# Moving the next layer's modulation set-up into the feed-forward of a four-layer, two-model transformer kernel

## The reference

```python
def first_block(...):
    s_lat, s_ctx = jax.nn.silu(c), jax.nn.silu(c_ctx)
...
    for i in range(DEPTH):
        mod = (s_lat @ w_mod[i] + b_mod[i])[:, None, :]
        sh1, sc1, g1, sh2, sc2, g2 = jnp.split(mod, 6, axis=-1)
        h = rms_norm(x, norm_mix[i]) * (1.0 + sc1) + sh1
        y, yc = token_mixers(h, hc, w_in[i], w_out[i], ...)
        x = x + g1 * y
        h = rms_norm(x, norm_ffn[i]) * (1.0 + sc2) + sh2
        x = x + g2 * swiglu(h, w_gate[i], w_up[i], w_down[i])
    return rms_norm(x, final_norm)
...
def second_block(...):
    for l in range(DEPTH):
        mod = c_act @ w_mod[l] + b_mod[l]
        sh_m, sc_m, g_m, sh_f, sc_f, g_f = jnp.split(mod, 6, axis=-1)
        h = rms_norm_2(x, mix_norm_pre[l]) * (1.0 + sc_m[:, None, :]) + sh_m[:, None, :]
        y = hybrid_mixer(h, ...)
        x = x + g_m[:, None, :] * rms_norm_2(y, mix_norm_post[l])
        h = rms_norm_2(x, ffn_norm_pre[l]) * (1.0 + sc_f[:, None, :]) + sh_f[:, None, :]
        x = x + g_f[:, None, :] * rms_norm_2(swiglu_2(h, w_gate_up[l], w_down[l]), ffn_norm_post[l])
```

## Time and profile before

| | us |
|---|---|
| median of 3 runs (lowest, highest) | 3956.61 (3956.02, 3957.63) |
| the profiled execution's own time | 3965.3 |
| its span, first to last instruction | 3963.5 |
| PE busy in the span | 3520.0 (89%) |
| mean granted TensorE clock in the span | 0.926 |

### The profile page before, as it was taken

One profiled execution on the slowest core, in us unless ns is written; L12 is line 12 of the kernel. 1 busy time (PEld: TensorE's weight loads), 2 busy tenths in 40 slices (PEclk: granted clock), 3 DMA queues, 4 the chain that ended last, 5 costly groups with the idle time before them and its releaser, 6 DMA issues. The chain is left out here.

```text
span 3963.5 us, 49063 instructions
## 1 busy us (share of the span) xinstructions
PE 3520.0 (89%) x20368; PEld 2899.2 (73%) x20368; DVE 1800.1 (45%) x3375; ACT 1058.1 (27%) x1717; POOL 10.7 (0%) x12
## 2 busy tenths in 40 slices
PE   6998998999997988999997974799997993799997
PEld 4987777888886976878875963468886882567886
DVE  3225654333335235544345447653334448654333
ACT  2112443111112222532222222532222322433222
POOL 0000000000000000000000000000000000000000
PEclk9997999999998987999998985899999996699998
DMA  5340101324241310134553310025443320012332
GB/s 190 124 149 1 47 23 53 112 80 136 72 136 45 86 54 25 33 106 149 154 152 104 93 54 1 1 61 173 138 144 122 100 81 0 1 43 85 96 99 72
DMA packets 318718, 336.52 MB, mean 85 GB/s; under 512 B 12025, under 2 KB 233761, under 8 KB 318497
## 3 DMA queue, kind: packets, MB, share of 16 engines
q1 hardware_dynamic: 318496, 333.38, 27.4%
HBM read 329.67 MB, written 3.67 MB: 84 GB/s over the span
## 5 line engine op out<-in xcount | busy, mean ns | idle before, releaser
L1369 DVE TENSOR_TENSOR weights_low<-weights,weights_high 128x1024 fp32r<-128x1024 f32 (+4 forms) x424 | 485.4, 1147 | 1289.4 <-ACT weights_high L1021 1287.5
L1021 ACT ACTIVATE weights_high<-weights 128x1024 fp32r<-128x1024 f32 (+4 forms) x424 | 422.2, 998 | 1421.6 <-PE banks L520 972.4
L917 PE MATMUL banks<-h_high,weights_high 128*128 128x512 f32 (+1 forms) x1760 | 658.4, 374 | 11.8 <-DVE h_low L1381 10.2
L917 PE MATMUL banks<-h_low,weights_high 128*128 128x512 f32 (+1 forms) x1760 | 650.0, 369 | 0.0
L917 PE MATMUL banks<-h_high,weights_low 128*128 128x512 f32 (+1 forms) x1760 | 648.8, 369 | 0.0
L520 PE MATMUL banks<-weights_high,h_high 128*128 128x426 f32 (+3 forms) x1424 | 516.7, 363 | 5.3 <-DVE h_low L1381 5.3
L520 PE MATMUL banks<-weights_high,h_low 128*128 128x426 f32 (+3 forms) x1424 | 509.5, 358 | 0.0
L520 PE MATMUL banks<-weights_low,h_high 128*128 128x426 f32 (+3 forms) x1424 | 509.1, 357 | 0.0
L917 PEld LDWEIGHTS banks<-h_high,weights_high 128*128 128x128 f32 x1760 | 332.8, 189 | 85.0 <-DVE h_low L1381 17.5
L917 PEld LDWEIGHTS banks<-h_high,weights_low 128*128 128x128 f32 x1760 | 332.9, 189 | 55.8
L917 PEld LDWEIGHTS banks<-h_low,weights_high 128*128 128x128 f32 x1760 | 333.2, 189 | 52.2
(11 more groups left out here) (253 smaller groups left out, 3922.3 us busy)
## 6 DMA issues: line engine op xcount, KB each, us to landing
projected<-in_w_mod SPq DMA_DIRECT2D x80, 1024.0 KB, 5.3
weights<-in_w_gate_up SPq DMA_DIRECT2D x88, 512.0 KB, 3.9
weights<-in_w_down SPq DMA_DIRECT2D x80, 512.0 KB, 3.9
weights<-in_w_in SPq DMA_DIRECT2D x80, 426.0 KB, 3.4
weights<-in_w_gate SPq DMA_DIRECT2D x44, 512.0 KB, 6.6
weights<-in_w_up SPq DMA_DIRECT2D x44, 512.0 KB, 7.7
weights<-in_w_mod SPq DMA_DIRECT2D x32, 512.0 KB, 3.9
weights<-in_w_out SPq DMA_DIRECT2D x32, 512.0 KB, 3.6
```

The source lines that it names most:

```text
L917: mm = pe.matmul(bank[:, 0:cnt], wt[:, k, :], x[:, k, a:a + cnt], start=(k == 0 and q == 0), stop=(k == KD - 1 and q == 2))
L1021: act.activation(WH[s_ % 2][:, 0:k * n], slots[j % LAND][:, 0:k * n], ACT.Copy).then_inc(S["w_high"], 1)
L1369: dve.tensor_tensor(WL[s_ % 2][:, 0:k * n], slots[split_of[s_] % LAND][:, 0:k * n], WH[s_ % 2][:, 0:k * n].bitcast(F32), ALU.subtract).the ...
```

## The change

For layers 0, 1 and 2 the kernel now also knows the layer that follows. SP issues the small loads of the following layer (`then_loads`) in the feed-forward, ahead of the first modulation tile. The bias is loaded straight into `ROWS`, and every tile is added to it. The 24 tiles are moved: two follow each of the blocks 0 and 1 (one after the gate product, one after the up product), one follows each later block, none the down product. After the first half of the last down product PE transposes the vectors, the columns and the first pair of gates of the following layer; DVE and ACT copy them out, DVE makes the scales. The second pair of gates is made in the next layer, beside its projection, into banks 6 and 7. So the head of layers 1, 2 and 3 has no small loads and no modulation work left.

The squares move too: behind the last residual adds of layers 0, 1 and 2, ACT squares each tile, and layers 1 and 3 and the final norm don't square at their start. Layer 2 still does, since the final norm changes the residual in front of it. `TMP` and `PO` get other places, with no other effect. Layer 0's head stays as it was. The core of the diff:

```diff
+    def loads(self, w, nxt, VR, BR, PO):
+        out = []
+        for name, a in self.at.items():
+            if a is not None:
+                v = w[name].rearrange("w (f p) -> (w f) p", p=PT)
+                out.append((VR[a:a + v.shape[0], :], v))
+        out += [(VR[self.next + 8 * i:self.next + 8 * i + 8, :], c.rearrange("a (f p) -> (a f) p", p=PT))
+                for i, c in enumerate(nxt["c"] if nxt else ())]
+        for q in range(4):
+            def quarter(v):
+                n = v.shape[-1] // 512
+                return v.rearrange("a (c q n) -> a q c n", q=4, n=PT)[:, q].broadcast_to([32, n, PT])
+            lane = slice(32 * q, 32 * q + 32)
+            out.append((BR[lane, :].rearrange("p (c n) -> p c n", n=PT), quarter(w["b_mod"])))
+            if self.second:
+                out += [(PO[lane, 256 * i:256 * (i + 1)].rearrange("p (c n) -> p c n", n=PT), quarter(w[n]))
+                        for i, n in enumerate(("post1", "post2"))]
+        return out
...
-    TMP = [SC[:, 2 * H_N + 512 * i:2 * H_N + 512 * (i + 1)] for i in range(2)]
+    TMP = [P[:, 4096 + 512 * i:4608 + 512 * i] for i in range(2)]
...
+                first_of_two = n == w["gate_up"][0][0] and a == w["gate_up"][0][1]
+                if m in (1, 2) and first_of_two:
+                    beside[len(weight_units) - 1] = 2 * m - 1
+                elif not first_of_two:
+                    beside[len(weight_units) - 1] = 2 * m if m < 2 else m + 2
         for half in range(2):
             for k in range(m0, m1, 2):
                 cols(w["w_down"], 512 * half, 512, k, min(k + 2, m1))
-            if m1 == KF:
-                beside[len(weight_units) - 1] = KF + half
...
+    def mods_of(m, by):
+        if not nxt:
+            return []
+        if m < 2:
+            return [2 * m + "ad".index(by)]
+        return [m + 2] if by == "d" else []
...
+    then_loads = then.loads(following["w"], following["nxt"], VR, ROWS, PO) if following else []
...
-            pe.wait_ge(S["small"], n_small)
             if start_loads:
+                pe.wait_ge(S["small"], n_small)
                 pe.wait_ge(S["constants"], 16)
-            bank = B.fill(pe, "d")
-            pe.transpose(bank[:, 0:nvec], VR[0:nvec, :], ident[0:nvec, 0:nvec]).then_inc(S["filled"], 1)
+                bank = B.fill(pe, "d")
+                pe.transpose(bank[:, 0:own.count], VR[0:own.count, :], ident[0:own.count, 0:own.count]).then_inc(S["filled"], 1)
...
+            def gates_beside(slot):
+                g = slot if slot < 2 else slot - 4
+                if not start_loads and slot in (0, 1, 6, 7) and g < 2 * R:
+                    if g < 2:
+                        B.free(pe, 6 + g)
+                    mod_gate(side.fill(pe, "a"), 10 + g // R, g % R).then_inc(S["side"], 1)
+            if start_loads:
+                mod_columns((0, 1, 2, 3))
...
-                    ready[m] = B.emptied_by("d")
-                    if nxt:
-                        mod_beside(m)
+                        if by == "d":
+                            ready[m] = B.emptied_by("d")
+                        for i in mods_of(m, by):
+                            mod_beside(i)
                 for half in range(2):
                     product(GH, GL, OUT_T, (m0, GOFF), 512, m0, m1, lambda i: "d", ready)
-                    if nxt and m1 == KF:
-                        mod_beside(KF + half)
+                    if following and (half, m1) == (0, KF):
+                        pe.wait_ge(S["then_loaded"], n_then)
+                        bank = B.fill(pe, "d")
+                        pe.transpose(bank[:, 0:then.count], VR[0:then.count, :], ident[0:then.count, 0:then.count]).then_inc(S["filled"], 1)
+                        pe.wait_ge(S["then_rows"], 1)
+                        mod_columns((0, 1, 2, 3), ROWS)
+                        mod_columns((6, 7, 8, 9), ROWS)
+                        for c in (4, 5):
+                            for r in range(then.rows):
+                                mod_gate(B.fill(pe, "a"), c, r, ROWS).then_inc(S["filled"], 1)
...
                     i = beside[j]
                     if i == 0:
                         sp.wait_ge(S["mod_room"], 1)
+                        for d_, s_ in then_loads:
+                            sp.dma_start(d_, s_).then_inc(S["then_loaded"], 16)
                     else:
                         sp.wait_ge(S["filled"], mod_release[i - 1])
...
-                    if which or i % 2:
+                    if which or i % 2 and not squares:
                         ins = act.activation(XNV[:, t, :], XV[:, t, :], ACT.Square, accum_out=ssq[:, i:i + 1])
-                ins.then_inc(S["squared"], 1)
+                if which or not squares:
+                    ins.then_inc(S["squared"], 1)
...
+                    g = i + 2 * (j - 1)
+                    if not start_loads and j in (1, 2) and i < 2 and g < 2 * R:
+                        bank = side.empty(act, "a", "a")
+                        act.activation(GBV[:, 1, g % R, g // R * 512:g // R * 512 + 512], bank, ACT.Copy).then_inc(S["side_kept"], 1)
...
+                    if following and (half, m1) == (0, KF):
+                        for _ in range(3):
+                            B.empty(act, "d", "a")
+                        mod_gates(range(1), then.rows)
+            if squares_after:
+                act.activation(nm[:, 0:1], ones_col, ACT.Sqrt)
+                for i, t in enumerate(OUT_T):
+                    act.wait_ge(S["x_final"], i + 1)
+                    act.activation(SC[:, D * i:D * (i + 1)], XV[:, t, :], ACT.Square, accum_out=ssq[:, i:i + 1])
...
-                if i % 2 == 0:
-                    copy_out(bank[:, 0:PT], rows)
-                    mod_first[0] = B.emptied_by("d")
-                else:
+                if i == 0:
+                    dve.wait_ge(S["then_loaded"], n_then)
+                elif i % 2:
                     dve.wait_ge(S["emptied_dve"], mod_first[0])
-                    dve.tensor_tensor(rows, rows, bank[:, 0:PT], ALU.add).then_inc(S["emptied_dve"], 1)
+                dve.tensor_tensor(rows, rows, bank[:, 0:PT], ALU.add).then_inc(S["emptied_dve"], 1)
+                mod_first[0] = B.emptied_by("d")
...
+                    for i in mods_of(m, "a"):
+                        mod_tile(i)
                     ahead()
...
+                    for i in mods_of(m, "d"):
+                        mod_tile(i)
+                if following and m1 == KF:
+                    dve.wait_ge(S["emptied_dve"], B.emptied_by("d"))
+                    if then.second:
+                        for i in range(2):
+                            g = ROWS[:, (4 + 6 * i) * PT:(6 + 6 * i) * PT]
+                            ins = dve.tensor_tensor(g, g, PO[:, 256 * i:256 * (i + 1)], ALU.mult)
+                        step(ins)
+                    dve.sem_inc(S["then_rows"], 1)
                 for half in range(2):
                     for k in range(m0, m1, 2):
                         ahead()
-                    outputs(1, half, more=m0 > 0)
-                    if nxt and m1 == KF:
-                        mod_tile(KF + half)
+                    outputs(1, half, m0 > 0, m1 == KF)
+                    if following and (half, m1) == (0, KF):
+                        bank = B.empty(dve, "d", "d")
+                        dve.tensor_copy(VT[:, 0:then.count], bank[:, 0:then.count]).then_inc(S["emptied_dve"], 1)
+                        mod_columns(0, MT_THEN)
+                        mod_columns(1, MT_THEN)
+                        mod_scales(0, then, MT_THEN, AT_THEN)
+                        mod_scales(1, then, MT_THEN, AT_THEN)
+                        for _ in range(2 * then.rows):
+                            B.empty(dve, "a", "d")
...
+        for l in range(2):
+            layer(nc, T, layers[l]["w"], S, False, l == 0, layers[l]["nxt"], start if l == 0 else (), layers[l + 1], l == 1, True)
+            end_of_layer()
...
+        for l in (2, 3):
+            layer(nc, T, layers[l]["w"], S, True, False, layers[l]["nxt"], (), layers[l + 1] if l == 2 else None, l == 3, l == 2)
```

More of the change, by code:

```diff
@@ L253, in layer @@
     PI32 = T["PI"]
[L255 to L258, removed]
+    own = Vectors(second, nxt)
+    then = Vectors(following["second"], following["nxt"]) if following else None
+    V_C, V_CC, V_N1, V_N2, V_QL, V_CB, V_CWT = (own.at[n] for n in ("c", "c_ctx", "norm1", "norm2", "q_latent_norm", "conv_b", "conv_w"))
+    V_NEXT, n_next = own.next, own.n_next
+    MT_THEN = AT_THEN = None
+    if following:
+        MT_THEN = SM[:, 272:272 + 32 * then.rows].rearrange("p (s k r) -> p s k r", s=4, r=then.rows)
+        AT_THEN = SM[:, 336:336 + 16 * then.rows].rearrange("p (s k r) -> p s k r", s=2, r=then.rows)
     weight_units = []
@@ L424, in spans @@
         return out + [(CTX_T * PT, LAT_T * PT, 0)]
[L427 to L442, removed]
+    small_loads = own.loads(w, nxt, VR, ROWS_IN, None) if start_loads else []
```

(43 more changed lines are left out.)

160 lines of the change are left out of this document (62 added, 98 removed).

## The result

The changed kernel takes 3927.47 us (median of 4 runs, 3924.18 to 3929.3), the kernel before 3957.12 (4 runs) beside it: a ratio of 0.9924, 95% interval 0.9911 to 0.9936, so 29.65 us or 0.75% faster. Forecast were 3930.5 and 26.1 us. The profiled execution took 3924.18 us (span 3922.4), 3.3 under its median, where the one of before stood 8.2 over the median beside it; the two spans are thus 41.1 us apart, and some 11.5 of that is no part of the change.

The account below looks back on a forecast made before the run. PE, busy 89% of the span, bounds the kernel. Heads gain 55.5 us, less 1.5, 8.0, 9.2, 6.5, 3.0 and 1.2, leaving 26.1: 3956.6 to 3930.5 us; range 3917 to 3947 (this case 3919 to 3944).

Parts of the forecast that it names:

- Heads: Starts of layers 1 to 3: transposes begin earlier and layer 1 loses a bank wait; 55.5 us gained in all.
- The warm-up: Eight dummy instructions of `warm(4)` opening each head, mostly at half clock: 6.6 us, bounds 3.6 and 7.2.
- A tie: Heads: second weight split done at 8.3 us, DVE's modulation begins at 8.2, so weights cost nothing; bound 2 us per head.
- The squares: Squares moved behind the last adds: about 1.1 us lost in three layers, 2.1 won in the final norm; net -1.2.
- Bank 6: Layers 2 and 3: first gate beside the projection waits for bank 6, 0.75 us each; -1.5 in all.
- Gates beside the projection: Four in layer 1, two each in layers 2 and 3, at 1.0 us each: -8.0.
- Halves: Set-up work between the halves of the last down product: 5.2 us in layer 0, 2.0 each in layers 1 and 2; -9.2.
- Tiles and their chain: Feed-forward blocks: two more tiles in each of three layers, -6.5; tiles 2 and 3 late in layers 1 and 2, -3.0.
- Cold start: Rival: clock falls back or never comes up before the projection, 4.2 us a head lost; 3943 us, chance 0.12.
- No change: Rival: weights replace small loads as the heads' last wait, some 7 us later than summed; 3955 us, chance 0.08.
- slower: Rival: tile and weight loads too slow in blocks 0 and 1 of layers 1 and 2; 3978 us, chance 0.05.
- 23.7 us of moved work: Work PE keeps outside the heads: gates beside the projection 8.0, between the halves 9.2, tiles 6.5.

Follow-up runs that it names:

- run 4: Changed kernel with vector transpose, columns, scales and all gates back in the layer heads; early loads, squares and tiles stay moved: 3932.45 us, ratio 0.9928.
- run 3: Changed kernel without the four dummy products at the start of the blocks of layers 1, 2 and 3: 3926.41 us, ratio 0.9915.
- run 2: Changed kernel with the first two gates beside the projection one slot later: 3924.89 us, ratio 0.9914.
- run 1: Changed kernel with the squares back in the heads and in the final norm: 3928.92 us, ratio 0.9924.
- run 5: As run 4, without the four head dummies, ACT's four gate copies behind modulation steps 2 and 4, layer 1 with four gates beside its projection: 3923.02 us.
- run 6: As run 5, also without the three dummy products between transposes and projection in layers 1 to 3: 3916.26 us, ratio 0.9879.
- experiment 7: Changed kernel again, no edit, in the rounds of run 5 and run 6, for a second profile: 3931.73 us, ratio 0.9917.

## Why the prediction was right, point by point

The mechanism held: each head lost its wait for the small loads, and PE paid for nearly all of the moved work. The 26.1 us lie inside the measured interval (25 to 35). By the steps:

- *Heads.* Forecast were transposes at 6.6 us and the first modulation at 8.2; measured 5.4, 5.5 and 5.1, and 6.8, 8.2 and 6.8. The warm-up was sized too near its upper end: the eight dummies took 5.2 to 5.5 us. The projection of layer 1 came 21.3 us into its block (22 forecast). "A tie" was the right reading of the place: DVE's second split ends just where the modulation starts. But only layer 3 waits for weights there; in layers 1 and 2 the splits queue behind ACT's scaling of the tiles.
- *The squares: the step that failed.* "In the heads of layers 1 and 3 it gains nothing, since `warm(4)` and the splits end last there" overlooked that layer 1 norms six tiles, and that ACT's table load of 1.28 us stands in that head. Its transposes would start at 8.5 instead of 5.4. The move was put at a loss of 1.2 and is a gain of 4.1 with the table load. The tails it lengthens cost 1.5, 1.3 and 1.2 (1.1 forecast); the final norm's block became 2.0 shorter (2.1). This did no harm to the sum, as the heads had been put at the times that hold with the squares moved.
- *Bank 6.* Found, and sized 0.75 instead of 1.2 in each of two layers.
- *Gates beside the projection.* 1.0 each forecast; in layer 1 four of them and the bank wait that vanished came to +1.7 together, so 3.9 or 0.97 each.
- *Halves.* 5.2 us forecast and 5.4 measured in layer 0. In layers 1 and 2 it was 1.0 and 1.5 instead of 2.0. Without the set-up work, layer 1's second half waits 1.23 us for a weight split (run 4), so part of that work was hidden.
- *Tiles and their chain.* 1.2 us for a tile (1.08 and the change of kind). The chain was put at 3.0: one wait of 1.2 in layer 2 is all that came, in both profiles of the changed kernel; it is 0.8 in run 3, 0.2 in run 2 and nothing in runs 1, 4, 5 and 6. The tile had landed 6.8 us after its issue, where its neighbours need 5.2 to 5.3. Why there alone is open.
- *Rivals.* Cold start: fallen by run 3 in its price, since each projection starts with the full clock. The falling back between the transposes and the projection that it named is there in layer 1, but there the kernel before has it too. The Trainium skill (TensorE: Matmul & The Clock Gate, Part 1: The HAM clock gate) has the throttled clock as the default, released by sustained activity. The rows agree: 0.53 over 2137.5 to 2141 in layer 2's head, full clock behind it; what I made of it was wrong, since in run 3 the clock rose during the transposes alone. No change and slower: the first weights were split from 3.7 to 5.3 us on, and the tiles of layers 1 and 2 landed in 5 to 7 us.

What the prediction did not see is that its two parts are not one: it charged 23.7 us of moved work as the price of the early loads. Of these, 17.2 are the gates and the work between the halves. Run 4 puts that work back into the head and is as fast, and run 6 shows that PE's idle time in the head hides most of it. The tiles' 6.5 stay in every run.

## What to carry to other kernels

When a head waits for small loads and then works on them, move the loads first and measure; the work may fit in for nothing where the engine waits for something else anyway, while between products of the bounding engine nearly all of it is paid. Dummy products that warm an engine up are a place to put real work; then look at the clock in each layer, since one of three here fell to half the clock in its first products without them. Before saying which of several waits ends last, count the tiles of each layer and look for what an engine does only once there, such as a table load.

## What the runs showed of the hardware

The clock rose 3.2 to 3.7 us after the block's start when PE ran dummies, about as late with the real set-up work (3.1 to 4.4 in runs 5 and 6), and 3.4 to 4.2 us after the first transpose where PE began with those (run 3): in these rows transposes alone, dummies and set-up work were followed by a rise about as soon. It fell back to 0.50 in the head of layer 1, in the changed kernel from 1267.0 to 1273.8, behind a stretch in which PE waited for DVE between groups of transposes. The Trainium skill (TensorE: Matmul & The Clock Gate, Part 1: The HAM clock gate) says that the number of slow products at a start is not fixed and varies between runs of one kernel. The windows 0.75 and 0.50 of experiment 7 show such a difference in the middle of a kernel. Two executions of one kernel can differ by 3.6 us in one mixer by the moment at which the clock rises; the four totals of run 5 reach from 3911 to 3927 us, so a difference of a few us is read from the places, not from two totals. In layer 3's projection the kernel before and run 4 ran 0.9% slower than the others at a granted clock of 1.00 (1.2 us over 139); no run tells why. ACT's table load took 1.28 us, and the root behind it started 0.02 us after its end (run 1, 1254.92 and 1256.22).
